# A bidirectional hybrid trunk: the two halves of each piece's squares are added by GpSimd before TensorE sums them over the rows

## The reference, cut to what matters

```
for l in range(DEPTH):                                   # 2
    mix = hybrid_mixer(rmsnorm(h, norm_mix_pre[l]), w_in[l], ..., w_out[l])
    h = h + rmsnorm(mix, norm_mix_post[l])
    ff = squared_relu_mlp(rmsnorm(h, norm_mlp_pre[l]), w_mlp_up[l], w_mlp_down[l])
    h = h + rmsnorm(ff, norm_mlp_post[l])
return h[:, N_META:]

def rmsnorm(x, g):
    return x * rsqrt(mean(x * x, axis=-1) + EPS) * g
```

## Time and profile before

| | us |
|---|---|
| median of 3 runs (lowest, highest) | 2224.91 (2224.6, 2225.53) |
| profiled execution, its own time | 2225.04 |
| its span in the trace | 2223.3 |
| PE busy | 2200.2 (99%) |
| PEld busy | 2002.1 (90%) |
| DVE busy | 1614.0 (73%) |
| ACT busy | 876.2 (39%) |
| POOL busy | 383.4 (17%) |

### The profile page before, as it was taken

The page is one execution under the profiler, slowest core; times in us unless marked ns, Lnnn a source line. Parts: engine busy times, 40 slices in busy tenths (PEclk is TensorE's granted clock), DMA queues, the critical chain, the costliest instruction groups (busy, mean ns, idle before and its releaser), DMA issues.

```text
span 2223.3 us, 34189 instructions
## 1 busy us (share of the span) xinstructions
PE 2200.2 (99%) x13864; PEld 2002.1 (90%) x13864; DVE 1614.0 (73%) x1621; ACT 876.2 (39%) x1031; POOL 383.4 (17%) x215
## 2 busy tenths in 40 slices
PE   8999999999999999999999999999999999999998
PEld 6999989999999999999989999887778888888888
DVE  6788634576877977977587886354768779778867
ACT  4564424352333342341255653242524433433415
POOL 3333215112000000002314332151220000000040
PEclk9999999999999999999999999999999999999999
DMA  3011102255654554551241111022566554643514
GB/s 143 34 55 37 39 20 96 74 209 206 241 186 147 211 186 175 172 194 71 90 141 43 53 39 39 20 96 75 208 220 225 194 182 152 245 177 139 194 57 152
DMA packets 122803, 291.01 MB, mean 131 GB/s; under 512 B 9552, under 2 KB 29264, under 8 KB 122704
## 3 DMA queue, kind: packets, MB, share of 16 engines
q1 hardware_dynamic: 56688, 166.24, 20.8%
q10 hardware_dynamic: 66016, 123.38, 16.2%
HBM read 251.51 MB, written 38.08 MB: 130 GB/s over the span
## 4 chain that ended last, share of the span: by engine, by line
PE 93%; DVE 3%; ACT 2%; issue 1%; DMA 1%; POOL 0%; SPq 0%; DVEq 0%; POOLq 0%
PE banks L763 34%; PE banks L1058 21%; PE banks L1028 21%; PE banks L901 5%; PE banks L815 3%; PE banks L818 1%; PE banks L1158 1%; PE banks L803 1%; PE banks L802 1%; PE banks L1165 1%; PE banks L1114 1%; PE banks L1135 1%; PE banks L1173 1%; DMA X<-t_mem 1%; PE banks L957 0%
## 5 line engine op out<-in xcount | busy, mean ns | idle before, releaser
L763 PE MATMUL banks<-X,w_hl 128*128 128x348 f32 (+2 forms) x3744 | 649.3, 332 | 0.0
L763 PEld LDWEIGHTS banks<-X,w_hl 128*128 128x128 f32 x3744 | 606.4, 188 | 25.6 <-issue 3.0
L664 POOL TENSOR_SCALAR w_hl<-w_raw 128x1024 fp32r<-128x1024 f32 x69 | 80.3, 1164 | 1628.3 <-PE banks L1058 949.2
L1028 PE MATMUL banks<-X,w_hl 128*128 128x260 f32 (+1 forms) x1944 | 311.7, 320 | 0.0
L1058 PE MATMUL banks<-sum_hi,w_hl 128*128 128x260 f32 (+1 forms) x1440 | 310.3, 320 | 0.0
L1028 PEld LDWEIGHTS banks<-X,w_hl 128*128 128x128 f32 x1944 | 277.9, 188 | 29.1 <-DVE Y L2353 0.4
L1058 PEld LDWEIGHTS banks<-sum_hi,w_hl 128*128 128x128 f32 x1440 | 223.5, 188 | 21.3
L668 POOL TENSOR_TENSOR w_hl<-w_raw,w_hl 128x1024 fp32r<-128x1024 f32 x69 | 204.3, 2960 | 5.8
L1058 PE MATMUL banks<-sum_lo,w_hl 128*128 128x260 f32 (+1 forms) x720 | 191.0, 319 | 0.0
L1686 ACT ACTIVATE sum_hi<-hid 128x1040 fp32r<-128x1040 f32 (+1 forms) x72 | 76.8, 1067 | 199.7 <-PE banks L1058 199.7
L2416 DVE TENSOR_TENSOR Y<-banks,Y 128x520 f32<-128x520 f32 (+1 forms) x144 | 122.1, 867 | 27.4 <-PE banks L1058 26.8
(11 more groups left out here) (257 smaller groups left out, 3622.1 us busy)
## 6 DMA issues: line engine op xcount, KB each, us to landing
w_raw<-w_units SPq DMA_DIRECT2D x148, 512.0 KB, 3.5
r<-w_units SPq DMA_DIRECT2D x82, 512.0 KB, 4.0
X<-t_mem ACTq DMA_DIRECT2D x44, 520.0 KB, 5.5
X<-t_mem ACTq DMA_DIRECT2D x44, 512.0 KB, 5.4
X<-t_mem SPq DMA_DIRECT2D x28, 520.0 KB, 5.4
X<-t_mem SPq DMA_DIRECT2D x28, 512.0 KB, 5.6
t_extra<-t_mem ACTq DMA_DIRECT2D x16, 520.0 KB, 4.4
t_extra<-t_mem ACTq DMA_DIRECT2D x16, 512.0 KB, 5.6
```

The costliest lines, as they stand in the source:

```text
L664: nc.gpsimd.tensor_scalar(slot[:, 0], w_raw[:, s], 1.0, 1.0, ALU.mult, ALU.mult).then_inc(w_rounded, 1)
L763: ins = nc.tensor.matmul(out[:, b, 0:t.width(b)], wp, xp[:, t.used(b)], start=first and n == 0, stop=last and n == 2)
L1028: ins = nc.tensor.matmul(banks[:, first + b, 0:t.block], wp, xp[:, b * t.block:(b + 1) * t.block], start=opens and (half, kk, i) == (0, 0, ...
```

## The change

In updates 1 to 3 POOL adds the second tile's squares of each piece onto the first's, in place, as soon as ACT has made them (`sq_h`), and counts them in `sq_added`. PE waits for `sq_added` and makes one product a piece. The start of the kernel stays as it was: the counts of `sq_added` go on from DVE's 12.

```diff
+            def add_halves(sbase, t):
+
+                for n in range(t.pieces):
+                    pool.wait_ge(sq_h, sbase + n + 1)
+                    pool.sem_inc(waited_pool, 1)
+                    halves = sq(t, n)
+                    nc.gpsimd.tensor_tensor(halves[:, 0, :], halves[:, 0, :], halves[:, 1, :], ALU.add).then_inc(sq_added, 1)
+
             for l in range(L):
 
                 if l > 0:
                     split(l, 0, 0, done(l - 1, j_down(GROUPS - 1, 1)), wslots[0])
+                    add_halves(l * 2 * NX, FULL)
                     pool.wait_ge(x_lo, l * X_PER + NX - 1)
...
                 split(l, U_MLP // 2 + 1, 0, done(l, J_O + 4), wslots[0])
 
+                add_halves(l * 2 * NX + NX, behind_mixer(l))
                 pool.wait_ge(x_lo, l * X_PER + NX + LT + HEADS + behind_mixer(l).pieces)
                 split(l, U_MLP // 2 + 1, 1, done(l, J_O + 5), wslots[1])
...
                 if first:
                     take_sum_bank(l, norm, b)
-                if sbase == 0:
-                    pe.wait_ge(sq_added, n + 1)
-                    nc.tensor.matmul(sum_bank(l, norm, b), ones[:, :], sq(t, n)[:, 0, :], start=first, stop=last)\
-                        .then_inc(sum_done if last else sq_read, 1)
-                    return
-                pe.wait_ge(sq_h, sbase + n + 1)
-                nc.tensor.matmul(sum_bank(l, norm, b), ones[:, :], sq(t, n)[:, 0, :], start=first, stop=False)
-                nc.tensor.matmul(sum_bank(l, norm, b), ones[:, :], sq(t, n)[:, 1, :], start=False, stop=last)\
+                pe.wait_ge(sq_added, sbase + n + 1)
+                nc.tensor.matmul(sum_bank(l, norm, b), ones[:, :], sq(t, n)[:, 0, :], start=first, stop=last)\
                     .then_inc(sum_done if last else sq_read, 1)
```

## The result

The changed kernel takes 2234.08 us (median of 6 runs, 2233.28 to 2235.35); the kernel before, run again beside it, takes 2225.57 (6 runs, 2224.6 to 2226.17). The ratio is 1.004, with a 95% interval of 1.0029 to 1.005: 8.5 us slower, where +8.3 and 2233.2 us were forecast. The profiled execution took 2234.01 us with a span of 2232.3.

A forecast was written before the change was run, and what follows sets the result against it. PE was taken to bound the kernel before, DVE's piece of 3.51 us the changed updates. Terms of +1.9, +4.2 and +2.2 sum to +8.3 us, 2233.2 us; own range 2229.5 to 2238, wider range 2222 to 2241.

The forecast's parts named there:

- DVE's margin of 0.2 us a piece: In the updates, PE's piece takes 3.08 us and DVE's 2.88, so DVE soon becomes the slower.
- rival 1: In the updates, DVE is not held back and POOL's latency bounds the end: -10.6 us, 2214.3 us; chance 0.14.
- The price of an add on DVE: In the updates, each POOL add lengthens DVE's chain by 0.63 us at 348 columns, 1.0 at 512.
- The edge: Overlap of a POOL add with DVE's instructions, taken off its cost to DVE: 0.23 us at 348 columns.
- rival 3: In the updates, each add blocks DVE fully, 0.86 and 1.31 us an add: 2240.1 us; chance 0.11.
- Rival 2: In the updates, most of an add falls in DVE's own gaps, 0.3 to 0.45 us: 2223 to 2228; chance 0.17.
- Update 1, forecast +1.9: Update 1's last product with the squares starts at 472.4 instead of 470.51, after eleven adds: +1.9 us.
- Update 2, forecast +4.2: Update 2's last product with the squares starts at 1159.0 instead of 1154.83, after eleven adds: +4.2 us.
- I give the first adds no idle time of DVE to fall in: In update 2 all eleven adds are charged to DVE at 0.63 us, 6.9 us.
- Update 3, forecast +2.2: Update 3's last product with the squares starts at 1582.2 instead of 1579.98, four adds costing 1.0 each: +2.2 us.
- DVE's 1.54 us of waiting: In update 3, DVE's wait for block 1's factor takes in two adds of 2.0 us together, leaving +0.46.
- About 2.0 us behind the high parts: At update 1's end, squares, DVE's low parts and POOL's add of 0.86 us delay PE's product that long.

The follow-up runs named there:

- e1: Kernel before, with one product a piece in updates 1 to 3 and no add, the second tile's squares left out; 2216.29 us, ratio 0.9957.
- e3: Changed kernel, with POOL memsets of a separate tile in place of each add, so POOL only writes; 2214.5 us, ratio 0.9951.
- e6: Kernel before, with squares and ones as fp32r in updates 1 to 3, both products kept, no add; 2213.41 us, ratio 0.9947.
- e2: Changed kernel, with POOL adding into a tile of its own and PE waiting for it, then making both products; 2235.84 us, ratio 1.0046.
- e4: Kernel before, with DVE making each add behind the piece's low parts and PE one product a piece; 2229.3 us, ratio 1.0017.
- e7: Kernel before, with fp32r squares and two products in updates 1 to 3 and at the start, DVE's adds there removed; 2210.86 us, ratio 0.9932.

## Why the prediction was right

**What bounds, and DVE's margin of 0.2 us a piece.** Right. With PE's work a piece cut (e1, e3, e6) the pieces come at DVE's 2.88 or 2.89 us and no faster. This is where half of the 20.9 us of PE's work went even with nothing held back: rival 1 priced that case at -10.6, and e3, which has POOL's latency and not its reads, measured 2214.5 against 2225.26, -10.8. That the rival's total fits is partly chance: it named POOL's latency as the bound, and e1, without it, has the same updates.

**The price of an add on DVE, 0.63 (348) and 1.0 (512).** Right, a little low: 0.68 (period 3.56 against 2.88) and 1.08 (line 1923's pair takes 2.50 at 512 columns where it took 1.42). The changed kernel's timeline in update 3, and the answer for line 695 alone (lengths in ns, min/median/max):

```profile
1572.35 2.50 DVE L1923 SCALAR_TENSOR_TENSOR Y<-Y,par,h_old 128x512 f32<-128x512 f32 x2
1572.35 1.28 POOL L695 TENSOR_TENSOR sq<-sq 128x512 f32<-128x512 f32 x1 [3.71 <-ACT sq L1312]
```

```profile
L695 POOL TENSOR_TENSOR sq<-sq x32: 936/1237/1671, 428.5 to 1587.3; 128x348 f32<-128x348 f32 x24, 128x512 f32<-128x512 f32 x8
```

POOL's add of 348 columns was taken to be 0.86 and is 0.94 where nothing is in its way (the median of 1.24 has the wait for a DVE instruction in it). The edge was taken as 0.23 and comes out as 0.94 - 0.68 = 0.26 at 348 columns and 1.28 - 1.08 = 0.20 at 512. So at 348 columns POOL's duration was 0.08 short and the edge right; at 512 the duration was right (1.31 against 1.28) and the edge, taken as 0.31, too wide. Full block (rival 3, by the Trainium skill, "SBUF — State Buffer", "Who interferes with whom") is right in kind and too dear in size: the trace leaves 0.2 to 0.26 us an add. Rival 2, the adds in DVE's gaps at 0.3 to 0.45, is out.

**Update 1, forecast +1.9, measured +1.42.** The last piece's new stream is done at 467.65 + 1.25 = 468.90, 5.9 us later within the update than before; 6.3 were forecast. Two of DVE's periods were 3.24 and 3.04 before, not 2.88 (scalings at 446.02, 449.26, 452.14, 455.18), small waits that I had left out and that took in some of the adds.

**Update 2, forecast +4.2, measured +3.48.** Eleven adds were priced at 0.63, 6.9 us; they cost 6.3. DVE's scalings from piece 1 to piece 11 took 33.60 us before and take 38.95. Nine adds cost 0.67 each. The first two cost 0.25 together, and here the step "I give the first adds no idle time of DVE to fall in" failed: idle time wasn't needed. The changed kernel's timeline of DVE and POOL:

```profile
1120.24 0.94 DVE L1873 TENSOR_TENSOR Y<-banks,Y 128x348 f32<-128x348 f32 x2
...
1120.24 0.94 POOL L695 TENSOR_TENSOR sq<-sq 128x348 f32<-128x348 f32 x1 [4.24 <-ACT sq L1312]
```

DVE's pair reads one operand from a PSUM bank and takes 0.94, as before (1117.34 0.94), beside an add that also takes its bare 0.94: both ran at once at full speed.

**Update 3, forecast +2.2, measured +2.91.** DVE's 1.54 us of waiting went as forecast (the period in which it stood was 5.53 and is 4.98). The term mis-sized is the add of 512: four at 1.08 instead of 1.0, and piece 0's, counted at nothing, cost 0.24.

**"About 2.0 us behind the high parts", because squares and POOL's add come after them.** The right size for the wrong reason. The product starts at 471.96, the high parts end at 469.43 + 0.57 = 470.00. But e1, with no add, shows the same 2 us through PE's own four low and eight high products behind the last low parts but one, and e3 shows that POOL's latency costs nothing. In the changed kernel the two end together: the add at 470.85 + 1.05 = 471.90, the product at 471.96. PE alone would be as late: its eight high products start at 470.67, and in e1 the product follows 1.25 us behind such a start (466.13 to 467.38), which gives 471.92. In update 3 the add is done at 1587.31 + 1.47 = 1588.78, 0.3 us before the product at 1589.08. So the sum was right although this step named POOL as the holder, where PE itself is as late or later.

**The sum.** +1.42 + 3.48 + 2.91 = 7.8 in the updates against the forecast 8.3, and about 1.1 outside them that the edits don't explain; medians are 8.5 apart. Parts of the agreement are luck: adds dearer by 0.05 to 0.08, the first two of update 2 nearly free, and the 1.1 us that no edit explains.

## What to carry to other kernels

Before moving work from the engine that bounds, read the next engine's period in the same stretch: PE's piece was 3.08 us and DVE's 2.88, so only 0.2 us a piece was to be had in the steady part, whatever PE was spared. An idle GpSimd is not free where DVE is that next engine and its instructions read two SBUF tensors: an add there cost DVE 0.68 us, more than the 0.43 that the same add costs when DVE makes it itself. Look first for a cheaper form of the same work on the same engine: `fp32r` squares, which are rounded, made both products together cheaper than the one that was to be saved. They gave 12.6 us, and 15.2 with the kernel's start, where the move lost 8.5.

## What the runs showed of the hardware

The hold of DVE by POOL is selective. Beside DVE's pair with two SBUF inputs, POOL reading two inputs (0.94 us) cost DVE 0.68, POOL reading one cost 0.22, POOL writing only (0.83 us of memsets) cost 0. Beside a DVE pair with one input in PSUM the two-input add cost nothing; e2 shows it once more (both 0.93 to 0.94 at 1120.6).

TensorE's granted clock fell for a moment near the end of update 3, where PE now has waits of up to 1.4 us. The changed kernel by windows (us; busy time and count of PE, PEld, DVE, ACT, POOL; granted clock as a share of full; DMA share; GB/s):

```profile
1570.00:1575.00 5.00, 3.34 (x11) 1.72 (x10) 4.96 (x6) 2.86 (x5) 1.28 (x1) 1.00 0.71 210
1575.00:1580.00 5.00, 2.78 (x8) 1.34 (x8) 4.96 (x6) 2.30 (x4) 1.27 (x1) 1.00 0.27 105
1580.00:1582.00 2.00, 0.79 (x2) 0.70 (x3) 2.00 (x3) 2.00 (x3) 0.00 (x0) 0.83 0.61 236
1582.00:1584.00 2.00, 2.00 (x6) 1.52 (x6) 1.96 (x2) 0.67 (x2) 1.28 (x1) 0.50 0.07 27
```

PE was busy 3.34 of 5 us, then 2.78 of 5, then 0.79 of 2, and was then granted 0.50, the level of 1.2 GHz, for about two microseconds. Two rows of its timeline show the price, eight high products at either level:

```profile
1582.14 3.22 PE L819 MATMUL banks<-X,w_out 128*128 128x512 f32 x8
...
1586.19 1.19 PE L822 MATMUL banks<-X,w_out 128*128 128x512 f32 x4
1587.22 2.02 PE L819 MATMUL banks<-X,w_out 128*128 128x512 f32 x8
```

3.22 us instead of 2.02. It cost nothing here, because PE's next step at 1586.19 waited for DVE's low parts in any case. Two other kernels had such a fall: e4 at 1577 to 1579, where what it cost wasn't separated, and e7 near the end of update 1. Windows and timeline of e7:

```profile
458.00:460.00 2.00, 1.99 (x7) 1.99 (x8) 1.96 (x4) 2.00 (x6) 0.00 (x0) 0.50 0.46 169
...
458.01 0.94 PE L821 MATMUL banks<-X,w_out 128*128 128x344 f32 x2 [1.34 <-DVE X L1887]
458.75 2.49 PE L818 MATMUL banks<-X,w_out 128*128 128x344 f32 x8
...
465.57 1.41 PE L818 MATMUL banks<-X,w_out 128*128 128x344 f32 x8
```

PE had waited 1.04 and 1.34 us for DVE's low parts, and the clock stood at 0.50 from 458 to 464. Eight high products took 2.49 us there instead of 1.41, and PE was never idle until the update's end, so this time was lost: update 1 took 31.34 us against e6's 29.58, though DVE was 3.2 us earlier to its last piece (457.87 against 461.10). The fall thus cost about 1.75 us. e6 had nearly the same waits (1.03 and 1.36 us) and no fall, so these runs don't show what decides. A gap opened on PE for another engine's sake can be charged a second time, if PE is the bound again right behind it.
